# A decoder layer on one core: squares summed in PSUM, single-column threshold steps, key halves, query blocks and joining factors made one step ahead

## The chip, the cores and the metric

The kernel runs on one core of one Trainium2 chip. The metric is the device time of one execution in microseconds (us), lower is better. TensorE is called PE in the profile, VectorE is DVE, ScalarE is ACT, GpSimd is POOL, and SyncE, which issues nearly all transfers, is SP.

## The reference, cut to what matters

One inference step of one decoder layer, for a prompt of 1024 tokens and for 8 samples of 8 new tokens with 4096 cached tokens each (1088 tokens in all). The model width is 1024, the inner width of the feed-forward parts 2816.

```python
x = x + 0.5 * swiglu(rms_norm(x, g_ffn1), w1_gate, w1_up, w1_down)
mixed, state = mixer(rms_norm(x, g_mix) @ w_in)      # attention with chosen keys, and a short convolution
x = x + mixed @ w_out
x = x + 0.5 * swiglu(rms_norm(x, g_ffn2), w2_gate, w2_up, w2_down)
gate = sigmoid(rms_norm(x, g_ple) @ w_ple_gate)
x = x + gate * (pe @ w_ple_proj)                     # and a last rms_norm
```

In the mixer, an indexer gives every token a score for every earlier key, and each token attends only to its 256 best keys:

```python
score = einsum('bth,bthl->btl', w, relu(logits))
score = where(adm, score, -inf)
_, idx = top_k(score, topk)
o = softmax(q . k[idx] / 8) @ v[idx]                 # 8 query heads, 2 key heads of 64
```

## The kernel before

All activations lie transposed in SBUF, features on partitions and tokens along the row. The 1088 tokens are cut into three chunks `c`: chunks 0 and 1 of 288 tokens (together group a, tiles `xa`, `xna`) and chunk 2 of 512 tokens (group b, `xb`, `xnb`). Every fp32 operand of a large product is split into a high half (`hi`, a rounding to fp32r that ACT makes with a copy) and a low half (`lo`, the rest, a subtraction on POOL, sometimes on DVE), and three matmuls (L1421 to L1423) form one product. So each 128x1024 weight tile costs ACT one copy (L828) and POOL one subtraction (L728) before PE can use it.

The order of the work is one list of events written by `Plan.order()`. Each engine walks through the same list and issues its own share of every event, so the list sets the order of every engine's queue, and each engine runs its queue strictly in order, waiting on semaphores. The large products are the list's backbone. `weave(main, groups, first, last)` hangs groups of small events behind the product parts ("p") `first` to `last` of the backbone, spread evenly. A product of a 288-token chunk has 2 such parts of 12 matmuls, one of the 512-token chunk has 4 parts of 6 matmuls. The stages, in time:

- feed-forward 1 for chunks 0 and 1 (to about 485 us), then the input projection of group a. Woven into it are the indexer scores of the samples (events `sil`, `siw`, with the head matrix `wm` that they need) and the search for the 256th score of prompt blocks 2 and 3: `threshold_bit`, 32 steps, one bit of the threshold per step. A step counts on DVE, for both blocks, how many scores reach the candidate (L1224), and builds the next candidate from the counts with instructions of two columns (L1236, L1238) and one column (L1241).
- feed-forward 1 for chunk 2, into which are woven the rest of the samples' search (`sample_bit`) and the prompt attention of blocks 0 to 3 (`prompt()`), and then the attention of the samples (`samples()`).
- the output projection, the input projection of group b, and feed-forward 2 for chunks 0 and 1, with the searches B1 and B2 (blocks 4 to 7) and their attention.
- the rest of feed-forward 2, the last gate, the last norm.

A norm is a chain over four engines: ACT squares 8 row tiles (L837, L841), DVE adds them up (L1039), PE sums over partitions (`sums`, L1513), ACT takes the root (L850), DVE inverts it and writes it on diagonals (L1044, L1051), PE spreads these (`spread`, L1526), DVE scales x (L1057), ACT and POOL split the result. `norm(..., apart=True)` returns this chain in groups for `weave`.

In the prompt attention one unit is a block `b` and a head `r`. Over three steps of the list a unit goes through `qk` (PE logits into PSUM bank 5, DVE maximum L1328, ACT exponential L959), `ptr` (PE transposes, ACT copies them to `PT`, L966; DVE inverts the row sum and writes it on the diagonal `dg`, L1344 and L1347), and `pv` (PE values, and `dg` spread by a matmul L1629). The query halves of a block come from event `qb` (ACT L951, POOL `qb_lo` L756), which stands directly ahead of the block's first unit:

```python
            if now and now[1] == 0:
                groups.append([("qb", now[0])])
```

In the samples' attention there is one slot for each 256 keys of a pair of samples, 68 in all: PE logits (`kq`), transposes (`vt`, L1666) and values (`vp`, L1685); ACT copies the transposes (`PTs`, L990), makes the key's high half (`ks`, `K_hi`, L976), and POOL the low half (`kv_kr`, L778). Within a slot the events are sorted by rank; `ks` has rank 4, behind the slot's logits and transposes. `vo` joins four chunks (softmax factors over diagonals `diag_s`, L1389, spread by PE L1697).

The rotary step of the input projection (`rotate`) multiplies the product z in its PSUM bank by the cosine into an SBUF tile `tb` (L1108, after which the bank is free), multiplies the half-swapped copy by the sine (L1111), and adds the two SBUF tiles (L1119). PE has 3 banks for products in turn.

## Time and profile before

| | us |
|---|---|
| median of 3 runs (lowest, highest) | 3026.08 (3020.22, 3026.2) |
| profiled execution, its own time | 3023.26 |
| span of the profiled execution | 3021.5 |
| PE busy in the span | 2636.0 (87%) |
| DVE, POOL, ACT busy in the span | 1427.7, 1008.3, 1005.3 |
| mean granted clock of TensorE over the span | 0.937 |

Times in rows are microseconds, durations of one instruction nanoseconds. A row that ends in a bracket names how long the engine had been idle before it and whose instruction ended that. The granted clock (PEclk) is TensorE's, as a share of full speed; at 1.0 it is 2.4 GHz, and a stretch is either at that or at half, 1.2 GHz, so 0.9 means a fifth of the stretch at half.

### The profile page before, as it was taken

How to read it: one execution, taken by the hardware profiler on the slowest of the kernel's cores; microseconds unless marked ns; L12 is line 12 of the kernel's file. 1: busy time of each engine (PE TensorE's matmuls, PEld its weight loads, DVE VectorE, ACT ScalarE, POOL GpSimd, SP SyncE). 2: the span in 40 equal slices, each digit the busy share in tenths (PEclk: the TensorE clock that was granted, in tenths of full speed). 3: DMA queues.
4: the chain of work that ended last, by engine and by line, in shares of the span. 5: the costliest groups of instructions: out<-in, count | busy, mean ns of one | idle time of the engine just before them, and what ended most of it. 6: DMA issues, size and time to landing. Idle time of an engine off the chain costs nothing. (4 is left out here: it accounts for less than half of the span.)

```text
span 3021.5 us, 41472 instructions
## 1 busy us (share of the span) xinstructions
PE 2636.0 (87%) x15166; PEld 2285.3 (76%) x15166; DVE 1427.7 (47%) x3227; ACT 1005.3 (33%) x1581; POOL 1008.3 (33%) x521
## 2 busy tenths in 40 slices
PE   4999998787887878888898966888999999999997
PEld 4999998566666666666786656777889988778887
DVE  3233324679774212222366787776333343442354
ACT  4222224422333233332345312333444233332242
POOL 4333333223223333333344222122122344454341
PEclk9999998898898889998998978998999999999999
DMA  4333234221111333433142111111111323223222
GB/s 144 96 103 97 92 102 133 100 78 56 63 50 49 104 111 102 124 119 100 61 143 72 63 51 49 43 49 43 43 55 58 105 77 98 90 93 105 91 70 74
DMA packets 157038, 253.40 MB, mean 84 GB/s; under 512 B 15010, under 2 KB 101283, under 8 KB 156835
## 3 DMA queue, kind: packets, MB, share of 16 engines
q1 hardware_dynamic: 154144, 247.02, 25.4%
q10 hardware_dynamic: 2690, 3.72, 0.3%
q8 instruction: 121, 1.98, 0.3%
q14 instruction: 83, 0.67, 0.1%
HBM read 240.34 MB, written 18.73 MB: 86 GB/s over the span
## 5 line engine op out<-in xcount | busy, mean ns | idle before, releaser
L728 POOL TENSOR_TENSOR w_lo<-raw,w_hi 128x1024 fp32r<-128x1024 f32 x250 | 603.3, 2415 | 1075.9 <-ACT w_hi L828 1075.4
L1421 PE MATMUL ps<-xna_hi,w_hi 128*128 128x288 f32 x2000 | 614.2, 307 | 38.1 <-DVE tb L1133 14.1
L1422 PE MATMUL ps<-xna_lo,w_hi 128*128 128x288 f32 x2000 | 602.2, 301 | 0.0
L1423 PE MATMUL ps<-xna_hi,w_lo 128*128 128x288 f32 x2000 | 601.7, 301 | 0.0
L1421 PEld LDWEIGHTS ps<-xna_hi,w_hi 128*128 128x128 f32 x2000 | 389.5, 195 | 52.9 <-DVE tb L1133 14.7
L1421 PE MATMUL ps<-xnb_hi,w_hi 128*128 128x512 f32 x1000 | 420.1, 420 | 10.8 <-DVE tb L1133 5.7
L1422 PE MATMUL ps<-xnb_lo,w_hi 128*128 128x512 f32 x1000 | 403.9, 404 | 0.0
L1423 PE MATMUL ps<-xnb_hi,w_lo 128*128 128x512 f32 x1000 | 402.8, 403 | 0.0
L728 POOL TENSOR_TENSOR d_lo<-raw,d_hi 128x1024 fp32r<-128x1024 f32 x90 | 216.5, 2426 | 532.5 <-ACT d_hi L828 532.5
L1422 PEld LDWEIGHTS ps<-xna_lo,w_hi 128*128 128x128 f32 x2000 | 389.0, 194 | 0.2
L1423 PEld LDWEIGHTS ps<-xna_hi,w_lo 128*128 128x128 f32 x2000 | 388.0, 194 | 0.0
L828 ACT ACTIVATE w_hi<-raw 128x1024 fp32r<-128x1024 f32 x250 | 263.5, 1054 | 200.0 <-PE ps L1423 117.3
L1421 PE MATMUL ps<-ha_hi,d_hi 128*128 128x288 f32 x704 | 216.8, 308 | 30.4 <-DVE xa L1165 24.4
L1421 PEld LDWEIGHTS ps<-xnb_hi,w_hi 128*128 128x128 f32 x1000 | 198.1, 198 | 57.6 <-issue 8.5
L1423 PEld LDWEIGHTS ps<-xnb_hi,w_lo 128*128 128x128 f32 x1000 | 196.4, 196 | 44.1
L1422 PEld LDWEIGHTS ps<-xnb_lo,w_hi 128*128 128x128 f32 x1000 | 197.9, 198 | 36.6
L1422 PE MATMUL ps<-ha_lo,d_hi 128*128 128x288 f32 x704 | 209.2, 297 | 0.0
L1423 PE MATMUL ps<-ha_hi,d_lo 128*128 128x288 f32 x704 | 208.9, 297 | 0.0
L1165 DVE SCALAR_TENSOR_TENSOR xa<-ps,xa 128x288 f32<-128x288 f32 x352 | 156.6, 455 | 109.3 <-PE ps L1423 108.9
L1165 DVE SCALAR_TENSOR_TENSOR xb<-ps,xb 128x512 f32<-128x512 f32 x176 | 121.5, 691 | 171.1 <-PE ps L1423 170.8
L828 ACT ACTIVATE d_hi<-raw 128x1024 fp32r<-128x1024 f32 x90 | 90.9, 1052 | 325.5 <-PE ps L1423 297.5
L1074 DVE TENSOR_TENSOR ps<-silu_a,ps 128x288 f32<-128x288 f32 x88 | 40.6, 462 | 290.6 <-PE ps L1423 276.8
(288 smaller groups left out, 4236.6 us busy)
## 6 DMA issues: line engine op xcount, KB each, us to landing
raw<-in_w_gu SPq DMA_DIRECT2D x176, 512.0 KB, 3.5
raw<-in_w_d SPq DMA_DIRECT2D x88, 512.0 KB, 3.5
raw<-in_w_ring SPq DMA_DIRECT2D x74, 512.0 KB, 3.5
pages<-in_vk_pages SPq DMA_DIRECT2D x256, 128.0 KB, 2.6
idx_flat<-in_idx_pages SPq DMA_DIRECT2D x256, 32.0 KB, 2.1
idxp<-idx_flat SPq DMA_DIRECT2D x8, 1024.0 KB, 8.1
x_spill<-xa SPq DMA_DIRECT2D x1, 2304.0 KB, 8.9
xa<-x_spill SPq DMA_DIRECT2D x4, 576.0 KB, 6.2
```

Of the source, the lines that this page charges most:

```text
L728: g_.tensor_tensor(lo[slot][:, :, :], raw[l % 2][:, :, :], hi[slot][:, :, :].bitcast(f32), ALU.subtract).then_inc(lo_done, 1)
L828: A(hi[slot][:, :, :], raw[l % 2][:, :, :], ACT.Copy).then_inc(hi_done, 1)
L1074: v.tensor_tensor(z, silu[g][:, own(c)], z, ALU.mult).then_inc(hmul_done, 1)
L1165: v.scalar_tensor_tensor(out=x[g][:, m, own(c)], in0=ps[:, 3 + (i - 1) % 2, 0:CH[c][1]], scalar=0.5, in1=x[g][:, m, own(c)], op0=ALU.mult, ...
L1421: mm(out, shi, mhi, start=first, stop=False)
L1422: mm(out, shi, mlo, start=False, stop=False)
L1423: return mm(out, slo, mhi, start=False, stop=last)
```

## The change

- `norm(..., apart=True)` returns an empty group between `sums` and `spread`, so `spread` falls one group later.
- `prompt()`: a block's `qb` stands at the fifth unit (r = 4) of the block before; for the first block it stands three groups ahead of its first unit.
- `samples()`: `ks` has rank -1, so the next slot's key halves are made ahead of the slot's own work; the joining factors of `vo` become events `vw` and `vf`, two and three slots behind the last logits of the four chunks, where `vo` stays at six.
- `wm` moves behind the indexer scores of blocks 2 and 3.
- The squares: ACT writes the first one into PSUM bank 5, DVE adds the next six there and writes the last sum to SBUF. Four of the 15 norms keep the old way (`in_psum`).
- The diagonal `dg` is written by ACT (a copy of the identity with a factor) ahead of its copy of the transposes.
- `rotate` multiplies by the cosine in place in PSUM and adds from there; PE takes the bank again after the whole step (`rope_done`).
- `threshold_bit`: the 128x2 instruction that makes the candidate with the next bit is gone, the comparison works on single columns; `sample_bit` needs one instruction less.

```diff
@@ -172,7 +172,7 @@
-        groups = [[("sums", k, c)], [("spread", k, c)] + [("scale", k, c, m) for m in range(4)], [("scale", k, c, m) for m in range(4, KT)]]
+        groups = [[("sums", k, c)], [], [("spread", k, c)] + [("scale", k, c, m) for m in range(4)], [("scale", k, c, m) for m in range(4, KT)]]
@@ -184,8 +184,10 @@
             pv = [("pv", *two)] if two else []
-            if now and now[1] == 0:
-                groups.append([("qb", now[0])])
+            if s == 0:
+                groups += [[("qb", now[0])], [], []]
+            elif now and now[1] == 4 and now[0] + 1 in blocks:
+                groups.append([("qb", now[0] + 1)])
@@ -206,13 +208,15 @@
                 if i < 4 and (ch, i) != (15, 3):
-                    put(s, (4, ("ks", *divmod(4 * ch + i + 1, 4))))
+                    put(s, (-1, ("ks", *divmod(4 * ch + i + 1, 4))))
                 put(end + 1 + i, (3, ("vt", ch, i)))
                 put(end + 2 + i, (1, ("vp", ch, i)))
                 slot["vp", ch, i] = end + 2 + i
             put(end, (1, ("smax", ch)))
             put(end + 1 + n, (2, ("ov", ch)))
             if ch % 4 == 3:
+                put(end + 2, (5, ("vw", ch // 4)))
+                put(end + 3, (5, ("vf", ch // 4)))
@@ -238,8 +242,8 @@
         first = weave(self.in_proj(0), self.norm(1, 1, True), 0, 2)
-        side = [[("iw", 0)], [("prep",), ("wm",)]] + [[("isc", 2, h, 0), ("isc", 2, h + 1, 0)] for h in (0, 2)]
-        side += [[("isc", 3, h, 0), ("isc", 3, h + 1, 0)] for h in (0, 2)] + [[("sil", 0)]]
+        side = [[("iw", 0)], [("prep",)]] + [[("isc", 2, h, 0), ("isc", 2, h + 1, 0)] for h in (0, 2)]
+        side += [[("isc", 3, h, 0), ("isc", 3, h + 1, 0)] for h in (0, 2)] + [[("wm",)], [("sil", 0)]]
@@ -351,8 +355,6 @@
                         add("rope", t, c)
-                        if t != T_IK:
-                            add("in_dve", e[1])
@@ -577,6 +579,10 @@
+        def in_psum(k, c):
+            return (k, c) not in ((1, 2), (2, 1), (4, 0), (4, 1))
@@ -827,14 +833,18 @@
+            added_up = [0]
             def square(k, c, m):
-                i = n("sq", k, c, m)
                 g = GROUP[c]
                 x_final(act, k, c, m)
                 if m == 0:
                     if k:
                         wait(act, sums_done, n("sums", k - 1, c))
-                    A(ssq[g][:, own(c)], x[g][:, m, own(c)], ACT.Square).then_inc(sq_done, 1)
+                    if in_psum(k, c):
+                        wait(act, ssq_done, added_up[0])
+                        added_up[0] = n("ssq", k, c, KT - 1)
+                    A(ps[:, 5, 0:CH[c][1]] if in_psum(k, c) else ssq[g][:, own(c)], x[g][:, m, own(c)], ACT.Square).then_inc(sq_done, 1)
@@ -961,6 +971,11 @@
                 o, k = page_groups(b)[i]
+                if i == 0:
+                    u = n("pv", b, r)
+                    act.wait_ge(ri_done, u)
+                    wait(act, pv_done, u - 2)
+                    A(dg[:, r % 2, :], ident[:, 0, :], ACT.Copy, scale=ri[:, r % 2:r % 2 + 1]).then_inc(dg_done, 1)
@@ -1036,7 +1051,8 @@
                     dve.wait_ge(ssq_done, n("ssq", k, c, m - 1))
-                v.tensor_tensor(ssq[g][:, own(c)], ssq[g][:, own(c)], sq[(q - 1) % 3][:, 0:CH[c][1]], ALU.add).then_inc(ssq_done, 1)
+                so_far = ps[:, 5, 0:CH[c][1]] if in_psum(k, c) else ssq[g][:, own(c)]
+                v.tensor_tensor(so_far if m < KT - 1 else ssq[g][:, own(c)], so_far, sq[(q - 1) % 3][:, 0:CH[c][1]], ALU.add).then_inc(ssq_done, 1)
@@ -1105,7 +1121,7 @@
                 if t != T_IK:
-                    v.tensor_tensor(zt[:, own(c)], z, cos, ALU.mult).then_inc(in_dve, 1)
+                    v.tensor_tensor(z, z, cos, ALU.mult)
@@ -1116,7 +1132,7 @@
                     dst = iqT[g][:, t, own(c)] if t < T_IK else zt[:, own(c)] if t == T_K else attn[g][:, t - T_Q, own(c)]
-                    v.tensor_tensor(dst, zt[:, own(c)], zs[:, own(c)], ALU.add).then_inc(rope_done, 1)
+                    v.tensor_tensor(dst, z, zs[:, own(c)], ALU.add).then_inc(rope_done, 1)
@@ -1232,14 +1248,12 @@
                 count(hits if name != "B1" else early_hits if j < EARLY else late_hits, blocks, cand[:, :].bitcast(f32), ALU.is_ge)
-                if j < 31:
-                    v.tensor_scalar(with_bit[:, :], cand[:, :], 1 << (30 - j), None, ALU.bitwise_xor)
-                dve.drain()
-                v.tensor_scalar(drop[:, :], reached[:, :], TOPK - 0.5, 1.0 if j else -1.0, ALU.is_lt, ALU.mult)
                 dve.drain()
                 for i in range(2):
-                    v.tensor_scalar(cand[:, i:i + 1], drop[:, i:i + 1], 31 - j if j else 0, (with_bit if j < 31 else cand)[:, i:i + 1],
-                                    ALU.logical_shift_left, ALU.bitwise_xor)
+                    v.tensor_scalar(drop[:, i:i + 1], reached[:, i:i + 1], TOPK - 0.5, float(2 ** (31 - j)) if j else -1.0, ALU.is_lt, ALU.mult)
+                dve.drain()
+                for i in range(2):
+                    v.tensor_scalar(cand[:, i:i + 1], drop[:, i:i + 1], 1 << (30 - j) if j < 31 else 0, cand[:, i:i + 1], ALU.bitwise_xor, ALU.bitwise_xor)
@@ -1278,10 +1292,11 @@
                 dve.drain()
-                v.tensor_scalar(s_other[:, :], s_other[:, :], s_reached[:, :], None, ALU.add)
+                v.tensor_scalar(s_drop[:, :], s_other[:, :], s_reached[:, :], TOPK - 0.5, ALU.add, ALU.is_lt)
                 dve.drain()
-                v.tensor_scalar(s_drop[:, :], s_other[:, :], TOPK - 0.5, 1.0 if j else -1.0, ALU.is_lt, ALU.mult)
-                dve.drain()
+                if j == 0:
+                    v.tensor_scalar(s_drop[:, :], s_drop[:, :], -1.0, None, ALU.mult)
+                    dve.drain()
@@ -1341,10 +1356,8 @@
                 dve.wait_ge(exp_done, u)
+                wait(dve, dg_done, u - 2)
                 v.reciprocal(ri[:, s:s + 1], rs[:, s:s + 1]).then_inc(ri_done, 1)
-                dve.wait_ge(ri_done, u)
-                wait(dve, pv_done, u - 2)
-                v.tensor_scalar(dg[:, s, :], ident[:, 0, :], ri[:, s:s + 1], None, ALU.mult).then_inc(dg_done, 1)
@@ -1377,9 +1390,11 @@
-            def sample_out(p):
+            def sample_lowest(p):
                 dve.wait_ge(s_nbias, 4 * p + 4)
                 v.tensor_reduce(s_low[:, :], s_nb[:, p % 2, :], axis=AX.X, op=ALU.min).then_inc(s_lowest, 1)
+            def sample_shares(p):
@@ -1388,6 +1403,8 @@
+            def sample_out(p):
@@ -1441,6 +1458,8 @@
                 elif kind == "in":
+                    if key[0] < T_V and key[0] != T_IK:
+                        pe.wait_ge(rope_done, n("rope", key[0], c))
```

On DVE, in search B1 (the threshold steps of blocks 4 and 5 inside feed-forward 2; `small_i` holds the candidates), one step and the start of the next stood like this before:

```order
L1224 TENSOR_SCALAR hits_late,small<-score_131,small_i 128x640
L1224 TENSOR_SCALAR hits_late,small<-score_132,small_i 128x768
L1236 TENSOR_SCALAR small_i<-small_i 128x2
L1238 TENSOR_SCALAR small_i<-small 128x2
L1241 TENSOR_SCALAR small_i<-small_i 128x1 x2
L1224 TENSOR_SCALAR hits_late,small<-score_131,small_i 128x640
```

and now, with the line numbers of the changed kernel:

```order
L1240 TENSOR_SCALAR hits_late,small<-score_131,small_i 128x640
L1240 TENSOR_SCALAR hits_late,small<-score_132,small_i 128x768
L1253 TENSOR_SCALAR small_i<-small 128x1 x2
L1256 TENSOR_SCALAR small_i<-small_i 128x1 x2
L1240 TENSOR_SCALAR hits_late,small<-score_131,small_i 128x640
```

The two instructions of two columns have become two of one column.

On ACT, in the samples' attention, where the exponential (`Sa`) of a chunk stands in the middle, the order before was:

```order
L990 ACTIVATE PTs_126<-ps 128x256
L976 ACTIVATE K_hi_124<-pages 128x512
L982 ACT_TABLE_LOAD
L982 ACTIVATE Sa_181,small<-Sa_181,small 128x1024
L990 ACTIVATE PTs_125<-ps 128x256
L976 ACTIVATE K_hi_123<-pages 128x512
```

and at a like place now:

```order
L1005 ACTIVATE PTs_126<-ps 128x256
L991 ACTIVATE K_hi_123<-pages 128x512
L997 ACT_TABLE_LOAD
L997 ACTIVATE Sa_181,small<-Sa_181,small 128x1024
L1005 ACTIVATE PTs_125<-ps 128x256
L991 ACTIVATE K_hi_124<-pages 128x512
```

The tile number shows the move: `K_hi_123`, the key half for the next slot, stood behind the exponential and the slot's transposes (`PTs_125`) and stands ahead of both. POOL's queue is the same in these slots, weight halves included.

On POOL, at the last block of the first prompt attention (`qs` are the samples' queries, `w_lo` and `d_lo` weight halves), before:

```order
L728 TENSOR_TENSOR d_lo_76<-raw_64,d_hi_74 128x1024
L761 MEMSET qs_f 128x768
L767 COPY qs_f<-attn_a 64x4x8 x16
L770 CAST qs_hi<-qs_f 128x768
L772 TENSOR_TENSOR qs_lo<-qs_f,qs_hi 128x768
L756 TENSOR_TENSOR qb_lo_173<-attn_a,qb_hi_169 128x512
L728 TENSOR_TENSOR w_lo_71<-raw_63,w_hi_67 128x1024
```

and now:

```order
L734 TENSOR_TENSOR w_lo_72<-raw_64,w_hi_68 128x1024
L762 TENSOR_TENSOR qb_lo_173<-attn_a,qb_hi_169 128x512
L734 TENSOR_TENSOR w_lo_69<-raw_63,w_hi_65 128x1024
L767 MEMSET qs_f 128x768
L773 COPY qs_f<-attn_a 64x4x8 x16
L776 CAST qs_hi<-qs_f 128x768
L778 TENSOR_TENSOR qs_lo<-qs_f,qs_hi 128x768
```

The block's query half has moved past the samples' queries and a weight half.

## Rows read from the trace of the kernel before

**Rows 1.** The page's head and its line of the granted clock in 40 slices.

```profile
span 3021.5 us, 41472 instructions
PE 2636.0 (87%) x15166; PEld 2285.3 (76%) x15166; DVE 1427.7 (47%) x3227; ACT 1005.3 (33%) x1581; POOL 1008.3 (33%) x521
...
PEclk9999998898898889998998978998999999999999
```

**Rows 2.** PE's waits, whole span: us in total, times, longest us.

```profile
PE ps L1421 <- POOL kv_kr L778: 75.5, 47, 10.4
PE ps L1421 <- DVE small L1328: 46.6, 24, 7.2
PE ps L1526 <- DVE diag L1051: 41.8, 9, 11.3
PE ps L1421 <- POOL qb_lo L756: 31.7, 5, 13.9
...
PE ps L1421 <- DVE tb L1133: 19.8, 5, 7.7
...
PE ps L1542 <- DVE WT L1192: 9.8, 1, 9.8
PE ps L1697 <- DVE diag_s L1389: 9.8, 4, 5.7
```

**Rows 3.** Stages: length, busy PE, PEld, DVE, ACT, POOL, clock, DMA, GB/s.

```profile
542.00:640.00 98.00, 86.54 (x456) 57.37 (x457) 65.83 (x229) 38.60 (x76) 14.65 (x7) 0.91 0.29 105
640.00:745.00 105.00, 84.10 (x540) 79.60 (x538) 93.95 (x218) 24.18 (x33) 39.68 (x19) 0.90 0.18 61
745.00:950.00 205.00, 159.67 (x700) 121.46 (x701) 151.85 (x390) 66.41 (x122) 59.71 (x43) 0.88 0.16 53
...
1020.00:1500.00 480.00, 388.22 (x1978) 310.44 (x1979) 104.59 (x312) 155.17 (x245) 162.87 (x99) 0.89 0.36 108
...
1735.00:2120.00 385.00, 300.49 (x1871) 273.77 (x1872) 295.31 (x745) 114.95 (x172) 84.73 (x36) 0.87 0.14 46
```

**Rows 4.** Timeline of slots in the samples' attention: start, length, instruction.

```profile
1196.78 0.62 ACT L976 ACTIVATE K_hi<-pages 128x512 fp32r<-128x512 f32 x1
...
1197.48 1.27 POOL L778 TENSOR_TENSOR kv_kr<-pages,K_hi 128x512 fp32r<-128x512 f32 x1 [3.58 <-ACT K_hi L976]
1198.89 0.36 PE L1421 MATMUL ps<-K_hi,qs_hi 128*128 128x256 f32 x1 [1.04 <-POOL kv_kr L778]
```

**Rows 5.** Timeline of such a slot with two down weights on POOL.

```profile
1231.79 4.70 POOL L728 TENSOR_TENSOR d_lo<-raw,d_hi 128x1024 fp32r<-128x1024 f32 x2 [8.06 <-ACT d_hi L828]
...
1237.85 0.36 PE L1421 MATMUL ps<-K_hi,qs_hi 128*128 128x256 f32 x1 [2.36 <-POOL kv_kr L778]
```

**Rows 6.** Timeline of DVE and POOL in search B1.

```profile
1780.68 2.40 POOL L728 TENSOR_TENSOR w_lo<-raw,w_hi 128x1024 fp32r<-128x1024 f32 x1 [25.93 <-ACT w_hi L828]
...
1781.49 1.62 DVE L1236 TENSOR_SCALAR small_i<-small_i 128x2 int32<-128x2 int32 x1
...
1783.43 0.34 DVE L1241 TENSOR_SCALAR small_i<-small_i 128x1 int32<-128x1 int32 x2
```

**Rows 7.** Groups by form: count, busy us, mean ns of one, idle before.

```profile
L1039 DVE TENSOR_TENSOR ssq_a<-ssq_a,sq 128x288 f32<-128x288 f32 x70 | 73.2, 1045 | 49.7 <-ACT sq L841 47.3
...
L1074 DVE TENSOR_TENSOR ps<-silu_a,ps 128x288 f32<-128x288 f32 x88 | 40.6, 462 | 290.6 <-PE ps L1423 276.8 <-ACT silu_a L869 12.9
...
L1236 DVE TENSOR_SCALAR small_i<-small_i 128x2 int32<-128x2 int32 x93 | 36.2, 389 | 0.0
...
L1241 DVE TENSOR_SCALAR small_i<-small_i 128x1 int32<-128x1 int32 x192 | 32.1, 209 | 8.7 <-issue 1.7
L1347 DVE TENSOR_SCALAR dg<-ident,small 128x128 f32<-128x128 f32 x64 | 31.2, 488 | 2.3
...
L1238 DVE TENSOR_SCALAR small_i<-small 128x2 int32<-128x2 f32 x96 | 29.8, 311 | 7.3
```

**Rows 8.** Timeline: a norm's spread inside feed-forward 2.

```profile
2582.68 1.65 PE L1526 MATMUL ps<-diag,ones 128*128 128x128 f32 x6 [4.93 <-DVE diag L1051]
```

More of the change, by code:

```diff
@@ L424, in program @@
         s_w, s_f = small[:, 28:32], small[:, 32:36]
-        cand, with_bit, drop = [small_i[:, 2 * j:2 * j + 2] for j in range(3)]
+        cand, drop = [small_i[:, 2 * j:2 * j + 2] for j in range(2)]
         s_cand, s_with_bit, s_drop = [small_i[:, 6 + j:7 + j] for j in range(3)]
@@ L1012, in _ @@
                     "sil": sample_logits, "siw": sample_scores, "vtr": values, "qb": queries, "qk": logits, "ptr": transposed,
-                    "ks": keys, "smax": weights, "vt": sample_transposed, "vo": shares, "mix": mix, "pe": embed}
+                    "ks": keys, "smax": weights, "vt": sample_transposed, "vw": shares, "mix": mix, "pe": embed}
             for e in events:
```

2 lines of the change are left out of this document (1 added, 1 removed).

## The prediction

> **What bounds the kernel now.** I first read the page's head and PE's waits. PE is busy for 2636.0 of 3021.5 us [rows 1]; it is idle for 385 us, and nothing else is near its bound, so time can only come from PE's idle time and from its clock. The waits say who holds PE up [rows 2]: POOL's key halves 75.5 us, the DVE maximum of the attention logits (L1328) 46.6, the diagonals of the norms 41.8, the query halves 31.7, DVE's convolution step (L1133) 19.8, the head matrix 9.8 and the joining factors 9.8. The stages [rows 3] say where: 92 us of idle time in the samples' attention (480 less 388.2), 85 in search B and its attention (385 less 300.5), 78 in 542 to 950. In the last two DVE is busy for 0.76 of the time (295.3 of 385, 311.6 of 408); in the samples' attention only for 0.22, so there it is a chain, not an engine's load. The clock [rows 1, 3] is the second loss: the granted clock of these stages is 0.87 to 0.91. At 0.89, a share of 0.22 of 480 us runs at 1.2 GHz, 106 us, and what PE does in it takes twice as long.
>
> **Key halves.** In an ordinary slot of the samples' attention, `K_hi` runs behind ACT's copy of the transposes (1196.78, 0.62), then POOL's `kv_kr` (1197.48, 1.27), and PE's next logits start at 1198.89, after 1.04 us of idleness [rows 4]. With `ks` ahead of the slot's own work, `K_hi` of the next slot runs behind the copy of the slot before, a whole slot earlier. Its key pages must be there (they come four slots ahead) and its buffer is free (its last reader is the slot before). PE's list of such stalls has 22 of 1.03 to 1.05 us, 4 of 1.74 or 1.75 where the exponential stands in the way, and 3 under 0.5: 31 us in all. The other 18 have another cause, which stays: POOL is at a weight. In [rows 5] two `d_lo` hold it until 1236.49, and `kv_kr` can't start earlier whatever ACT does; PE still waits its 2.36. There are 9 of these (2.36 to 3.42, 23 us), 8 of 1.27 to 1.53 behind one `w_lo`, and the first, 10.4, waits for the first pages. I take 31 off; the bounds are 20 (pages come late where slots get shorter) and 45 (half of the `w_lo` and `d_lo` ones go too).
>
> **Joining factors.** `vw` and `vf` now stand three to four slots ahead of their spread; slots are near 5 us. The 9.8 us go but for 1: 8.5, bounds 4 and 10.
>
> **Norms.** `spread` falls later behind `sums`: by one part of 6 matmuls in the two norms of the first input stage of group b, by 12 in the one before, and in feed-forward 2 from 18 matmuls to 36 and to 48. A matmul of 512 columns at full clock takes 0.21 us, so that is 1.3, 1.3, 2.6, 3.8 and 6.4 us of cover. [rows 8] is one of two stalls of 4.93 us. I take off 1.3 + 2.6 + 3.8 + 4.9 = 12.6, bounds 8 and 16. The norms at both ends of the kernel have no product between, and the second one of the first input projection only moves its wait to the scaled tiles.
>
> **Head matrix.** Five groups later its 9.8 us are covered; some of it may come back as a wait for the indexer keys, since these loads don't start earlier. 9, bounds 0 and 10.
>
> **Query halves.** Of 31.7 us [rows 2], the longest, 13.9, is block 4's; it gets two groups more (some 4 us), but its `qb_hi` on ACT stands behind a product that waits for DVE's tie steps. The other four, 17.8 in sum, belong to blocks that now have four units' lead, one of them past the samples' queries on POOL (the order above). 4 + 15 = 19, bounds 12 and 28.
>
> **DVE's threshold steps and diagonals.** The 128x2 instructions take 389 and 311 ns on average, the 128x1 209 [rows 7]. [rows 6] shows why the averages are high: L1236 takes 1.62 us and ends as POOL's `w_lo` ends (1783.08). The Trainium skill (SBUF — State Buffer, "Who interferes with whom") says that DVE and GpSimd share a port pair under an exclusive lock, which a tensor_scalar in a two-port mode takes and one outside it doesn't; the trace agrees as far as L1241, which is never slow. So a step saves 0.39 + 0.31 less the 0.34 of a pair of single columns [rows 6], 0.36, and with 96 steps 35 us, of which I put three quarters in search B, where it has 64 of the steps and POOL is at weights beside them. The samples' search loses one single-column instruction, 0.21 x 32 = 7. `dg` takes 0.49 from DVE in each of 64 units; blocks 0 to 2 are in 745 to 950 (24 units, 12 us), blocks 4 and 5 in search B's stage (16 units, 8 us). So DVE is lighter by 9 + 7 + 12 = 28 us before 950 and by 26 + 8 = 34 in search B. PE's idle time there was 78 and 85 us [rows 3]. Not all of DVE's gain arrives, since PE and DVE take turns in waiting: I take 20 and 25 (near three quarters), bounds 7 and 9 (a quarter), and 28 and 40 (all, with the drains that go).
>
> **What costs or gains nothing.** `dg` on ACT costs 64 instructions of some 0.3 us in a queue that is busy for 0.32 in 745 to 950 [rows 3]; DVE itself took 0.49 [rows 7]; it waits for the reciprocal, which DVE makes right behind the maximum that ACT's exponential needs anyway, and PE needs the transposes only one unit later. The squares: 77 adds with one operand from PSUM should go from 1045 ns (L1039, [rows 7]) to the 462 of L1074, 45 us of DVE; but they lie in stages in which PE is full, and only the last sums wait for them, 3 us (bounds 0 and 5). The Trainium skill speaks against this step (VectorE: DVE Perf Modes, "The TRN2 errata — SBUF-src ops pay a fixed extra latency per instruction": 120 against 58 cycles of fixed cost for a PSUM source). By it the 77 adds would take 5 us more, on nobody's path; the row of L1074 shows no such price. The rotary step holds PE's bank for two DVE instructions more, some 1 us of the two products (6 us) until PE is back at it; its third instruction loses its contention, in a stage in which PE is full.
>
> **Clock.** These terms take 128 of 385 us of idleness, a third. The granted clock of 0.937 over the span means some 380 us at 1.2 GHz, and it falls where PE stalls: slices 1 to 6 of the page's line, feed-forward 1, hold 9. If a fifth of these 380 us returns to 2.4 GHz, PE saves half of it: 39, bounds 12 and 75.
>
> **Sum.** 31 + 8.5 + 12.6 + 9 + 19 + 20 + 25 + 3 + 39 = 167. The profiled execution took 3023.26 us with a span of 3021.5; the median is 3026.08. 3026 - 167 = 2859. All the low bounds together give 72 (2954), all the high ones 257 (2769).
>
> **Rivals.** (1) The stalls are handed on: what DVE and the key halves no longer hold up waits for the next in line, POOL's weights (L728 stands in front of `kv_kr` and `qb_lo` alike), DVE's tie steps, or the key pages on SP. For it: POOL's weights are what PE waits for in [rows 5]. Then the key halves, the joining factors and the head matrix keep 31 + 8 + 9, DVE brings a quarter (16), the clock 12, the rest 10: 86, 2940. Against it: in [rows 4] nobody but the chain itself is late, and POOL had been idle for 25.93 us ahead of the weight in [rows 6]. (2) The clock returns further. If it comes back for half of the 380 us, that is 95 instead of 39, and all of DVE's gain arrives (+17): 167 + 56 + 17 = 240, 2786. Against it: the stalls behind weights remain, 34 us in the samples' attention alone. (3) Slower: `dg` holds up ACT. ACT's queue is in order; if the reciprocal stands behind a threshold step of DVE (two counts and their tail, near 2.7 us in search B), `PT`, the silus and the weight copies behind `dg` all wait. At 2.7 us for each of 64 units that is 173, and 64 x 0.3 = 19 for the copies: 167 - 192, so 3051. It decides from (167 - 19) / 64 = 2.3 us a unit up; against it stands the order above: in the list the reciprocal follows the maximum directly, and the threshold step is ahead of both. (4) The change does not do what it says on DVE: single columns still take the port, PSUM adds are no faster. Then 45 and 3 are gone, and with them 8 of the clock: 111, 2915, inside my range.
>
> **Chances and range.** My forecast 0.74, rival 1 with rival 4 0.16, rival 2 0.07, rival 3 0.02, no difference 0.01. Two runs of this kernel can differ by 0.2% (6 us), which is about what a measurement can tell from no change. Cases 1, 2 and 4 are all faster. Faster by over 0.2%: 0.96, within 0.01, slower 0.03. The range 2768 to 2950 takes in rivals 1, 2 and 4 and leaves out little more than the ends of the bounds.
>
> **What the changed profile would show.** The wait of PE for `kv_kr` at 45 us, all of 1.2 us and more; for `diag_s` under 2; for `qb_lo` near 13; no stall of 4.93. The squares' adds near 0.46 us, the new single-column instructions at 0.15 to 0.21 with no slow ones, DVE's busy time down by some 120 to 1300 us. Mean granted clock near 0.95. The forecast is wrong if the samples' attention (480 us [rows 3]) is not shorter by 40 or more with the clock, or if search B's stage (385) does not lose 45; and if PE's waits show a new name, ACT's `PT` or `rope_done` above all.

## The result: 2951, where 2859 was predicted

The changed kernel takes 2951.43 us (median of 4 runs, 2947.79 to 2952.68), the kernel before 3026.14 (4 runs); ratio 0.9755, 95% interval 0.9738 to 0.9772. That is 75 us faster where 167 was predicted, and 1.4 us outside the range. The page of the changed kernel, to compare with [rows 1]:

```profile
span 2946.0 us, 41473 instructions
...
PE 2630.5 (89%) x15166; PEld 2293.6 (78%) x15166; DVE 1307.1 (44%) x3135; ACT 1020.3 (35%) x1641; POOL 1010.6 (34%) x521
...
PEclk9999998999889989888999988999999999999999
```

PE's idle time fell from 385.5 to 315.5 us, by 70 (the prediction took 128 off). PE's busy time, in which a faster clock would show, fell by 5.5 where 39 was forecast: over the span the time at 1.2 GHz went from 379 to 349 us, where 76 was to go. DVE lost 121 us, as foretold. PE's waits, to compare with [rows 2]:

```profile
PE ps L1438 <- POOL kv_kr L784: 59.2, 21, 10.3
PE ps L1438 <- DVE small L1343: 54.6, 15, 13.3
PE ps L1545 <- DVE diag L1067: 43.7, 12, 11.2
...
PE ps L1438 <- DVE tb L1149: 11.6, 4, 5.5
...
PE ps L1438 <- POOL qb_lo L762: 3.4, 1, 3.4
...
PE ps L1586 <- DVE Wm L1214: 1.2, 1, 1.2
```

Names have gone or shrunk (`diag_s` is no longer there, `WT` neither, `qb_lo` was 31.7), but the DVE maximum rose from 46.6 to 54.6, the diagonals by 2, and `kv_kr`, forecast at 45, stands at 59: fewer stalls (21 for 47) that are longer each (18 of the 21 take 2 us or more, 10 of the 47 did).

These stages are cut at the same instruction in both kernels: the prompt attention of blocks 0 to 3, the samples' attention, and the stage from group b's input projection to the end of search B's attention, before (length, busy PE, PEld, DVE, ACT, POOL, clock, DMA share, GB/s):

```profile
752.06:1029.07 277.01, 228.33 (x1040) 174.50 (x1040) 169.60 (x433) 95.27 (x165) 80.00 (x52) 0.90 0.18 57
1029.07:1527.70 498.63, 413.78 (x2103) 331.48 (x2103) 123.06 (x333) 166.90 (x261) 170.11 (x100) 0.91 0.36 110
...
1613.48:2441.98 828.50, 729.68 (x4417) 638.71 (x4417) 501.31 (x1179) 295.45 (x433) 225.00 (x98) 0.94 0.18 59
```

and after:

```profile
751.54:1009.42 257.88, 224.79 (x1022) 172.35 (x1022) 145.42 (x365) 105.45 (x197) 85.48 (x52) 0.90 0.19 61
1009.42:1489.48 480.06, 419.14 (x2103) 346.02 (x2103) 125.38 (x333) 163.96 (x259) 169.59 (x100) 0.88 0.38 114
...
1575.29:2368.88 793.59, 718.04 (x4411) 629.53 (x4411) 437.79 (x1146) 300.12 (x459) 223.68 (x98) 0.95 0.19 61
```

Two of these cuts moved with the change itself: block 0's first logits and group b's first `spread` now stand 18 and 6 weight matmuls further down the list (x1040 became x1022, x4417 x4411). So blocks 0 to 3 lost 19 in these rows, but with the stage ahead of them, which got 4 longer, 15; search B lost 35, or 32 between the same weight matmuls. The stretch of 1735 to 2120, for which the prediction asked 45, lost 26 by that cut (383.5, then 357.1), and the samples' attention 19, where 40 was the mark. In that last one PE idles 24 us less (84.9, then 60.9) and is busy for 5 us more with the same 2103 matmuls, at a lower clock (0.91, then 0.88).

**The key pages.** The prediction let `K_hi` be read a slot earlier on the ground that its pages "come four slots ahead". ACT's waits before, and after, say what that did:

```profile
ACT K_hi L976 <- DMA pages<-in_vk_pages: 15.4, 8, 7.3
```

```profile
ACT K_hi L991 <- DMA pages<-in_vk_pages: 84.9, 25, 7.2
```

One such case in the changed kernel's timeline (start, length, instruction, idle time before it; the last row is another slot, for the clock below):

```profile
1047.61 0.34 SPq L609 DMA_DIRECT2D raw<-in_w_gu  x1
1053.26 8.66 SPq L692 DMA_DIRECT2D pages<-in_vk_pages  x12
...
1058.01 0.63 ACT L991 ACTIVATE K_hi<-pages 128x512 fp32r<-128x512 f32 x1 [5.57 <-DMA pages<-in_vk_pages]
...
1058.71 1.27 POOL L784 TENSOR_TENSOR kv_kr<-pages,K_hi 128x512 fp32r<-128x512 f32 x1 [8.66 <-ACT K_hi L991]
...
1060.12 0.36 PE L1438 MATMUL ps<-K_hi,qs_hi 128*128 128x256 f32 x1 [2.19 <-POOL kv_kr L784]
...
1206.91 0.36 PE L1438 MATMUL ps<-K_hi,qs_hi 128*128 128x256 f32 x1 [2.36 <-POOL kv_kr L784]
```

SP issues a weight transfer at 1047.61, when POOL is done with that buffer, then reads the 16 page numbers of the next chunk into registers, and only at 1053.26 issues the first page: over 5 us in which SP issues no transfer. ACT stands at `K_hi` for 5.57 us, POOL is idle for 8.66, PE waits 2.19.

The kernel before shows that there was little room. By its list a key tile's pages are issued three slots ahead of its logits in 44 of 60 cases, not four: the transfer waits until PE is done with the values of the tile eight before it, which have the same buffer. And in its trace the pages of the first key tile after a reading of page numbers had landed 0.9 us before `K_hi` began (medians, the first eight tiles left out), those of the other three 3.6 to 5.9 us. A slot takes some 6 us. In the changed kernel these are 0.0 and 1.2 to 2.9, and 63 of the 73 us that ACT waits for these tiles stand at the tiles behind a reading.

**The clock.** Before, a stall of 1.04 us at 1198.89 [rows 4] left the clock alone:

```profile
1191.00:1197.80 6.80, 5.06 (x29) 3.70 (x27) 0.72 (x3) 2.46 (x6) 1.58 (x2) 1.00 0.43 126
1197.80:1205.00 7.20, 5.12 (x33) 4.01 (x32) 1.88 (x5) 2.36 (x4) 2.22 (x2) 1.00 0.26 75
```

After, the clock fell behind the stall of 2.36 us that ends at 1206.91:

```profile
1200.00:1204.50 4.50, 4.50 (x28) 3.53 (x26) 0.77 (x3) 3.14 (x5) 3.65 (x2) 1.00 0.10 13
...
1208.00:1214.80 6.80, 6.80 (x26) 5.65 (x26) 0.51 (x3) 0.39 (x1) 0.00 (x1) 0.53 0.24 73
```

From 1208.00 to 1214.80 the granted clock is near its lower level (1.2 GHz) and PE needs the whole stretch for 26 matmuls, where it had 28 in 4.5 us; those of 512 columns, which had followed each other by 0.23 us, now do so by 0.43. I counted PE's stalls in the samples' attention and a little around it, cut at the same weight matmuls: before, 42 of 0.8 to 2 us and 12 of 2 us or more, with 102 us at 1.2 GHz; after, 7 and 19, with 123 us. Below, "the stage" is this cut.

### The profile page after: what moved, and what is told of

Same layout as the page of the kernel before. It is cut to its first block, busy times and chain, and to the rows that moved or that the text cites. A ratio compares the mean times of both kernels' runs of the same rounds, so it can differ in the third digit from the quotient of the medians.

```text
span 2946.0 us, 41473 instructions
## 1 busy us (share of the span) xinstructions
PE 2630.5 (89%) x15166; PEld 2293.6 (78%) x15166; DVE 1307.1 (44%) x3135; ACT 1020.3 (35%) x1641; POOL 1010.6 (34%) x521
## 4 chain that ended last, share of the span: by engine, by line
PE 69%; DVE 15%; ACT 4%; issue 4%; POOL 3%; DVEq 2%; DMA 2%; SPq 1%; ACTq 0%
PE ps L1438 21%; PE ps L1439 19%; PE ps L1440 19%; PE ps L1646 2%; PE ps L1704 2%; POOL w_lo L734 2%; DVE hits L1240 1%; PE ps L1632 1%; DVE hits_early L1240 1%; DVE ps L1090 1%; DVE s_hits L1288 1%; ACT w_hi L834 1%; DVE ha_lo L1092 1%; PE ps L1573 1%; DVE tb L1154 1%
## 5 line engine op out<-in xcount | busy, mean ns | idle before, releaser
L1438 PE MATMUL ps<-ha_hi,d_hi 128*128 128x288 f32 x704 | 215.6, 306 | 22.2 <-DVE xa L1181 21.1
```

The lines of the kernel that those rows point to most:

```text
L1438: mm(out, shi, mhi, start=first, stop=False)
```

## Experiments

18 kernels, four or five runs each (12 of k_alone, 11 of n_before), beside the kernel before on the same chip (its medians there are 3026.5 to 3027.3). "Faster" and "slower" are against the changed kernel's 2951.4 unless another is named. The 95% intervals are 4 to 7 us wide to either side for most kernels, so a difference under some 6 us is not told from none. Idle is span less PE's busy time in the profiled execution, which is one of the runs and not always near the median.

| kernel | median (range) | PE busy | PE idle | mean clock |
|---|---|---|---|---|
| changed | 2951.4 (2947.8-2952.7) | 2630.5 | 315.5 | 0.941 |
| u_keys | 2953.0 (2949.5-2955.9) | 2625.4 | 328.7 | 0.944 |
| u_steps | 2988.2 (2968.0-2997.4) | 2627.7 | 338.5 | 0.940 |
| u_dg | 2959.7 (2947.6-2960.4) | 2632.8 | 325.3 | 0.940 |
| u_norm | 2949.5 (2941.2-2950.9) | 2631.9 | 317.2 | 0.939 |
| u_qb | 2952.9 (2937.9-2960.4) | 2638.8 | 319.7 | 0.938 |
| u_psum | 2966.6 (2964.3-2969.0) | 2640.2 | 322.3 | 0.938 |
| u_joins | 2964.4 (2961.0-2965.7) | 2634.3 | 328.3 | 0.936 |
| k_alone | 3017.8 (3011.6-3027.8) | 2645.6 | 370.9 | 0.933 |
| n_before | 3018.4 (3016.7-3021.1) | 2632.4 | 382.7 | 0.939 |
| n_after | 2929.2 (2927.3-2929.7) | 2615.3 | 312.5 | 0.945 |
| f_weights | 2940.0 (2935.9-2942.6) | 2618.8 | 322.1 | 0.941 |
| f_numbers | 2912.7 (2911.6-2922.5) | 2610.3 | 310.4 | 0.944 |
| k_numbers | 2972.1 (2965.9-2979.6) | 2616.9 | 347.2 | 0.947 |
| f_all | 2913.8 (2909.6-2916.8) | 2616.8 | 298.0 | 0.945 |
| f_late | 2947.8 (2944.6-2949.8) | 2639.1 | 307.8 | 0.939 |
| f_pages | 2980.4 (2979.2-2981.3) | 2624.9 | 353.7 | 0.936 |
| f_hold1 | 2960.0 (2950.9-2962.7) | 2609.4 | 348.9 | 0.940 |
| k_weights | 2984.3 (2980.8-2985.6) | 2624.4 | 359.0 | 0.941 |

### One part undone at a time

**u_keys.** 

> The changed kernel with the rank of ks put back from -1 to 4, all else as changed (2951). My theory: key halves one step ahead removed only the stalls of 1.04 and 1.75 us, and these cost no clock, while the stalls behind POOL's weights grew, so the edit is worth what the waits say: kv_kr goes from 59 back to about 75, 16 us, 2967 (2961 to 2973). Rival: the edit brought its full 31 us and something else took 15 away: 2982. Rival: the stalls behind weights simply take over, nothing is gained: 2951 to 2955.

```diff
-                    put(s, (-1, ("ks", *divmod(4 * ch + i + 1, 4))))
+                    put(s, (4, ("ks", *divmod(4 * ch + i + 1, 4))))
```

1.5 us slower, no difference: in the range of the last rival. Idle time rose by 13, PE's wait for `kv_kr` is back at 74.9 as I expected, and busy time fell by 5; the stage has 38 short stalls, 11 of 2 us or more and 92 us at 1.2 GHz, for 123. The waits said 16, the time says nearly nothing: the theory had the waits right and the price wrong, since with the edit undone 8 long stalls go too, and with them 31 us at 1.2 GHz.

**u_steps** (`threshold_bit` and `sample_bit` as before). 

> The changed kernel with the old instructions of two columns in threshold_bit and the old sample_bit. DVE gets 35 + 7 us busier. As the prediction priced it (three quarters arrive): about 30 us, 2981. My theory now: PE's idle time in search A and B hangs on DVE only in a few places (the first logits of block 4, of block 0, some maxima), so a third to a half arrives: 12 to 20 us, 2963 to 2971. Rival: DVE's slower steps are hidden and nothing arrives: 2951 to 2956.

37 slower in the median, above all I expected. The five runs spread over 29 us, with mean clocks from 0.940 down to 0.932; the profiled one is the fastest of them (2968.0), and its span is 20 above the changed kernel's, 23 more of idle time and 3 less of busy time. So 23 is what the profile shows of waiting, and how much of the 37 is the clock is not shown by a trace. PE's waits for `tb` and the DVE maximum, 11.6 and 54.6, are 19.6 and 67.3.

**u_dg** (`dg` on DVE as before). 

> The changed kernel with the diagonal dg written by DVE again. DVE gets 31 us busier (64 x 0.49). Priced in the prediction as three quarters of 12 + 8 us in the places where PE waits for DVE, 15 us less what ACT's copies cost: 2961 to 2966. Rival: DVE is not the last there and ACT's dg costs PE something (its waits for ACT's PT are 14 us): 2945 to 2951.

8 slower, with runs from 2947.6 to 2960.4; idle time rose by 10, as PE's wait for the maxima did (54.6, then 65.2).

**u_norm.**

```diff
-        groups = [[("sums", k, c)], [], [("spread", k, c)] + ...
+        groups = [[("sums", k, c)], [("spread", k, c)] + ...
```

> The changed kernel without the empty group in norm(), so spread falls where it fell before. Prediction's term: 12.6. By the two profiles (diagonals 41.8 before, 43.7 after; 4.93 became 3.58, 4.93 became 1.44, 4.49 became 2.48, but 3.74, 1.90 and 1.40 are new or moved) I now expect 5 to 8 us of idle time, 2954 to 2960. Rival: the full 12.6, 2964. Rival: nothing, the empty group only moves the waits: 2948 to 2953.

Nothing lost, as the second rival said. Undone, the two stalls of [rows 8]'s kind are back:

```profile
2511.53 1.65 PE L1545 MATMUL ps<-diag,ones 128*128 128x128 f32 x6 [4.93 <-DVE diag L1067]
...
2606.72 1.38 PE L1545 MATMUL ps<-diag,ones 128*128 128x128 f32 x6 [4.93 <-DVE diag L1067]
```

In the changed kernel they are shorter by 4.8, but the norm at 2806 has a stall of its own that u_norm lacks:

```profile
2508.05 1.65 PE L1545 MATMUL ps<-diag,ones 128*128 128x128 f32 x6 [3.58 <-DVE diag L1067]
...
2599.78 0.94 PE L1545 MATMUL ps<-diag,ones 128*128 128x128 f32 x6 [1.44 <-DVE diag L1067]
...
2806.41 2.08 PE L1545 MATMUL ps<-diag,ones 128*128 128x128 f32 x8 [3.74 <-DVE diag L1067]
```

DVE's rows ahead of that stall say why:

```profile
2796.36 0.18 DVE L1060 RECIPROCAL rstd<-rstd 128x4 f32<-128x4 f32 x1 [0.77 <-ACT rstd L860]
2802.78 0.46 DVE L1102 TENSOR_TENSOR ps<-silu_a,ps 128x288 f32<-128x288 f32 x1 [6.24 <-PE ps L1440]
...
2803.66 2.70 DVE L1067 TENSOR_SCALAR diag<-ident,rstd 128x128 f32<-128x128 f32 x4
```

The empty group moved not PE's `spread` alone but DVE's share of the event too: the diagonals, for which all was ready at 2796.54, now stand behind the additions of the next product, which wait for PE for 6.24 us. The prediction's list of norms did not have this one. Three more got worse with the empty group: at 501 a stall of 1.28 is 3.73, and those of 1.40 at 1497 and 1.90 at 2897 are new. In all PE waits 43.7 us for these diagonals, 39.8 with the group gone.

**u_qb** (`qb` directly ahead of the block's first unit). 

> The changed kernel with qb put back ahead of each block's first unit, and without the two empty groups. The four query halves at 745 to 950 (17.8 us before, gone after) come back, the one of block 4 (13.9) only changes its name (13.3 + 3.4 after, for DVE and for qb_lo). Theory: 15 of the prediction's 19 are real, 2963 to 2970. Rival: DVE's maxima take them over (PE's wait for small rose by 8): 2955 to 2960.

1.5 slower, and the runs go from 2937.9 to 2960.4, so no difference can be read. The rival's mechanism is there, though not its 4 to 9 us: most of what goes from one line comes up on the other (63.4 together, 58.0 in the changed kernel):

```profile
PE ps L1436 <- DVE small L1341: 31.9, 14, 7.0
PE ps L1436 <- POOL qb_lo L760: 31.5, 5, 13.9
```

**u_psum** (`in_psum` always false). 

> The changed kernel with all sums of squares in SBUF again. DVE gets 77 x 0.5 = about 40 us busier where PE is full. Prediction's term: 3, so 2954. Rival: nothing, 2949 to 2953. Rival: the late norms (diagonals, and the sums at the kernel's ends) gain more from it than I gave them: 2958 or more.

15 slower, the third case: the profile has 7 us more of idle time and 10 more of busy time, with 369 us at 1.2 GHz in the span for 349.

**u_joins** (`vw`, `vf` and `wm` at their old places). 

> The changed kernel with the joining factors and the head matrix at their old places. PE's waits for diag_s (9.8) and WT (9.8, now Wm 1.2 and rl 2.1) come back: idle time up by 15 to 18, 2966 to 2970 if the clock stays. Rival (their gain was given to the next in line): 2951 to 2957.

13 slower, a little under what I expected, with 13 more of idle time. `diag_s` (10.8) and `WT` (9.9) are back.

The seven differences (1.5, 37, 8, -2, 1.5, 15, 13) add up to 74 of the 75 us. With some 5 us of noise in each that is no proof that they act independently, and the key halves below show that one of them does not. The rotary step was not tried alone.

### The key halves and SP

**f_pages.** Two edits of SP's queue (from both, cut to what matters): it reads the next chunk's numbers right behind the last pages of this one, and it keeps a weight's transfer back until the slot's pages are issued, which puts 28 of this stage's 29 weight transfers behind one more slot's pages:

```diff
-                if k % 4 == 0:
+                if k == 0:
                     numbers[:] = page_numbers(4 * k, 16)
...
+                if k % 4 == 3 and k < 63:
+                    numbers[:] = page_numbers(4 * k + 4, 16)
...
+                if e[0] == "sp" and ks_seen and numbers:
+                    pending.append(e)
...
+                if pending and (e[0] == "kl" or not ks_seen):
+                    for q in pending:
+                        does["sp"](*q[1:])
```

> The changed kernel (2951), only SP's queue in the samples' attention altered: the pages' transfers of a slot are issued ahead of the weight transfers that fall into it, and the 16 page numbers of a chunk are read as soon as the registers are free. Theory C (the key halves gain nothing because K_hi, read a slot earlier, waits for its pages: ACT's wait for pages rose from 15 to 85 us with the change, and the halves made late then meet POOL's weights): ACT's wait for pages falls under 30, PE's wait for kv_kr from 59 to about 45, the time by 10 to 15 with it: 2936 to 2941. Rival A (POOL's weights in front of kv_kr alone): ACT's wait falls, PE's does not, 2948 to 2954. Theory D, on the clock, holds beside either: what PE's idle time loses in this stage comes back for the most part as time at 1.2 GHz, so the gain is under half of the idle time saved.

29 slower, outside both ranges. ACT's wait for pages fell to 36, but ACT now waits 56 us for the raw weight (`d_hi`), and PE's wait for `kv_kr` rose to 84. SP issues pages and weights from one queue, and here the one that stood behind came late.

**f_hold1** (as f_pages, a weight's splitting a slot later). 

> As f_pages, and the splitting of a weight in this stage stands a slot later in the list, behind the next slot's keys and pages, so that POOL's kv_kr does not stand behind it and ACT's d_hi does not block K_hi. If the two causes together (pages late, weights in front) make up all that the key halves should have brought, PE's wait for kv_kr falls to 10 to 20 (10 is the first), idle time by 40, and the time is 2911 without help of the clock, 2890 if the clock returns with it, and 2930 or more if theory D holds (the clock takes back half or more).

9 slower. PE's wait for `kv_kr` did not fall to 20 but rose to 93; raw weights are late again (61 us), and the stage idles 104 us in fewer and longer stalls.

**k_weights** (as f_pages, keys at rank 4, a weight's splitting behind `ks`). 

> As f_pages, but the keys at their old rank (4), and the weights' splitting behind the slot's ks. Then every slot has the short stall of about 1.04 us (some 45 us in all with the first), no long one behind a weight, and the pages have their full lead. Theory D (long stalls and work without pauses both bring PE to 1.2 GHz, short stalls do not): PE's idle time is about that of the changed kernel less 15 to 25, with less time at 1.2 GHz in the stage than its 115 us: 2925 to 2940. Rival (the key halves a step ahead are worth their 31 us once pages and weights are out of the way): slower than f_hold1 by 20 or more.

33 slower. It is 24 behind f_hold1, as the rival said, which speaks for a worth of the keys' lead once the queues are out of its way. Every variant that puts pages ahead of weights on SP lost against the changed kernel.

**f_weights.** The splitting (with its next transfer) stands behind the next `ks`; on SP only 4 of the stage's 29 weight transfers fall behind one more slot's pages:

```diff
-            out.append(("sp", len(self.items) - 1))
+            (held if holding else out).append(("sp", len(self.items) - 1))
...
             out.append(e)
+            if e[0] == "ks":
+                out += held
+                held, holding = [], e[1:] != (15, 3)
```

> The changed kernel, but in the samples' attention a weight's splitting (ACT w_hi and d_hi, POOL w_lo and d_lo) is written into the list behind the next ks instead of ahead of it, so kv_kr no longer stands behind a weight that PE itself has just released. Theory A (queue order is the cause of what was left of the key halves): PE's wait for kv_kr falls from 59 to about 15, of which the first 10 stays; 44 us of idleness go, 2907, and if the clock returns for half of the stage's 115 us at 1.2 GHz, another 25: 2880. Rival B (the weights themselves are the late ones, POOL's work in a slot doesn't fit in PE's): the wait changes its name to d_lo or w_lo and the time stays within 10 us: 2941 to 2960.

11 faster, neither theory: PE's wait for `kv_kr` is 55 and not 15, idle time rose by 7, busy time fell by 12, and ACT's wait for pages rose to 135 us. Theory A, that POOL's order alone was the cause, fell here.

**k_alone** (the kernel before, `ks` at rank -1, nothing else). 

> The kernel before (3026) with the key halves' edit alone (rank -1). Theory C: ACT's wait for pages rises from 15 to 80 or more, the stalls of 1.04 us go, stalls of 2 us and more go from 12 to about 19 in this stage, and the time hardly moves: 3018 to 3028. Rival (prediction's term, if nothing else of the change disturbed it): 2995.

9 faster than the kernel before (ratio 0.9974, 0.9963 to 0.9986), not 31. PE's wait for `kv_kr` and ACT's for the pages:

```profile
PE ps L1421 <- POOL kv_kr L778: 59.9, 20, 10.4
...
ACT K_hi L976 <- DMA pages<-in_vk_pages: 80.0, 26, 7.3
```

The stage has 143 us at 1.2 GHz for 102, 19 stalls of 2 us or more for 12, and 9 shorter ones for 42. So the pages were late by this edit alone, and nothing else of the change was needed to take most of the gain away.

**n_after** and **n_before**: the four lines on the page numbers above, alone, in the changed kernel and in the one before. 

> The changed kernel (2951) with the early page numbers alone. Theory C: the pages come some 5 us earlier once in four keys, ACT's wait for pages falls from 85 to about 60, two or three of the 19 long stalls go: 2930 to 2944. Rival (only both edits together help, the weights stand in front): 2947 to 2953.

 

> The kernel before (3026) with the early page numbers alone. Theory C: its keys are made a slot later and find their pages there (ACT's wait for pages is 15 us in all), so nothing changes: 3020 to 3029. Rival (SP is late for everything, weights too): 3010 or less.

22 faster in the changed kernel; in the one before 8 faster than that kernel, a little more than the nothing that I expected (ratio 0.9974, 0.9965 to 0.9983), with 3 us less of idle time. SP's order of transfers is the same in n_after as in the changed kernel. Its waits:

```profile
PE ps L1440 <- POOL kv_kr L786: 49.8, 17, 10.4
...
ACT K_hi L993 <- DMA pages<-in_vk_pages: 59.1, 27, 7.3
```

**f_numbers** (f_weights and the page numbers). 

> f_weights (2940) with one thing more: SP reads the 16 page numbers of the next chunk right behind the last pages of this one, instead of ahead of the next pages (it spends 5 us on them each time, and K_hi waits: ACT's wait for pages is 135 us in f_weights). Theory C, SP's queue is what the key halves now wait for: ACT's wait for pages under 90, PE's wait for kv_kr from 55 to 25 to 35, 2915 to 2930 with the clock as it is. Rival (theory D has the upper hand): idle time falls, the time by less than half of it: 2930 to 2938. Rival (SP is not it): 2938 to 2942.

39 faster than the changed kernel, ratio to the kernel before 0.9624 (0.961 to 0.9637): the stage is down to 10 stalls of 2 us or more and 87 us at 1.2 GHz.

```profile
PE ps L1445 <- POOL kv_kr L791: 34.4, 11, 10.7
...
ACT K_hi L998 <- DMA pages<-in_vk_pages: 100.4, 30, 7.6
```

Faster than I expected, though ACT's wait is not under 90. It is PE's that counts: against n_after, whose only difference is the order of the splitting, PE's wait for `kv_kr` is 15 less and the time 17.

**k_numbers** (f_numbers with `ks` back at rank 4). 

> f_numbers (2913) with the rank of ks put back from -1 to 4. Theory C: the term of 31 us was right for a kernel whose pages are in time. Then the stalls of 1.04 us come back, some 40 us in all, without as many long ones: 2935 to 2945. Rival (the keys' lead never mattered, f_numbers gains by SP's numbers alone): 2910 to 2918.

59 slower than f_numbers. PE waits 92 us for `kv_kr`, and the stage has 40 stalls of 0.8 to 2 us. Neither range held. The 59 is not the keys' lead alone: this kernel is also 19 slower than u_keys, from which it differs by the early numbers and the splitting, and at this rank the splitting follows directly on the keys. u_keys with the early numbers alone was not tried. If they gave it the 8 that they gave the kernel before, it would take 2945, and the lead would be worth 16 against n_after; that is an estimate, and the lead's own worth is not shown.

### Block 4's first logits

The stall of 13.29 us, where 13.9 for `qb_lo` had been, in the changed kernel:

```profile
1799.72 0.56 DVE L1278 TENSOR_SCALAR score<-score 128x768 f32<-128x768 f32 x1
...
1800.54 1.15 DVE L1240 TENSOR_SCALAR_CACHE_REDUCE hits<-score,small_i 128x896 bf16<-128x896 f32 x1
...
1814.07 0.33 DVE L1256 TENSOR_SCALAR small_i<-small_i 128x1 int32<-128x1 int32 x2
...
1814.52 0.49 DVE L1343 CUSTOM_DVE_ANT_0 Sx_b<-ps,score 128x320 f32<-128x320 f32 x1
...
1815.07 0.63 PE L1438 MATMUL ps<-kT_hi,qb_hi 64*128 64x320 f32 x1 [13.29 <-DVE small L1343]
```

The tie steps end at 1800.28, and then four steps of search B2 run before the maximum (the rows show the first count and the last step's end): three of them were given the place of `qb` and of the two empty groups behind it.

**f_late.**

```diff
-            side.append((late[i] if i < len(late) else []) + g)
+            side.append((late[i - 4] if 4 <= i < len(late) + 4 else []) + g)
```

> The changed kernel, but search B2's steps start four groups later, so that no threshold step stands between the tie steps of search B1 and the first logits of block 4 on DVE (now four stand there, some 13 us). Theory: PE's stall of 13.3 us at 1815 shrinks to about 2, and with it goes some of the 20.5 us at 1.2 GHz there: 2951 - 11 - 8 = 2932; a part comes back as blocks 4 and 5 see four steps more later: 2932 to 2943. Rival: the logits wait for the tie steps anyway, nothing changes: 2948 to 2953.

4 faster, less than the range and within the noise. The 300 weight matmuls around block 4's first logits take 10 us less, but the 300 around 2020 take 8 more: B2's tie steps for block 6 now stand ahead of the last maximum of block 5, and PE has a stall of 7.00 us at 2025.99. Idle time fell by 8, busy time rose by 9. **f_all** (f_numbers with two groups instead of four). 

> f_numbers (2913) with search B2's steps two groups later, so that two threshold steps instead of four stand between B1's tie steps and the first logits of block 4. The stall of 13.3 us shrinks by 6, and by f_late (8 us of idle time less brought 4): 2905 to 2911. Rival: the steps come to stand ahead of block 6 and cost there what they save: 2911 to 2915.

No difference to f_numbers, as its rival said: the medians are 1 us apart. The profile has 12 us less of idle time and 6 more of busy time, but f_numbers' profiled run is the slowest of its five (2922.5).

## Why the prediction was wrong

- **Key halves: 31 forecast, 2 measured.** The failing step is "Its key pages must be there (they come four slots ahead)". By the kernel's own list they come three slots ahead of the logits in 44 of 60 cases, and the first tile behind a reading of page numbers had 0.9 us to spare where the move asked for a slot, some 6. I named pages as a low bound (20) and read no wait of ACT or of SP for it. The 22 stalls did vanish; the halves came late by another way, behind SP and then behind POOL's weight, as stalls of over 2 us. k_alone shows it without the rest of the change: 9 us instead of 31, ACT's wait for pages 80 instead of 15. That SP had its part is shown by n_after (22 us from the page numbers alone, against 8 in the kernel before, whose keys are made later); that the order of the weights had its part, by f_numbers against n_after (17 us).
- **Clock: 39 forecast, 5.5 of busy time measured.** "It falls where PE stalls" was right, "if a fifth of these 380 us returns to 2.4 GHz" had no ground: 30 us returned. The idleness that went was for the most part in short stalls, behind which the clock had not fallen. In 14 of the profiles together (the two kernels and the twelve variants that were run first), I counted the stalls near which time at 1.2 GHz began, from 1 us ahead of the stall to 4 us behind it:

  | stall, us | stalls | with a fall of the clock |
  |---|---|---|
  | 0.8 to 1.2 | 340 | 30 |
  | 1.2 to 2 | 225 | 75 |
  | 2 to 2.5 | 167 | 140 |
  | 2.5 to 4 | 312 | 275 |
  | 4 to 6 | 110 | 109 |

  Seen from the other side, 615 of the 706 falls stand at a stall of 2 us or more and none away from every stall (two stand at one under 0.8), so the half of theory D by which work without pauses would bring the clock down too is not borne out.
- **Query halves: 19 forecast, 1.5 measured, and norms: 12.6 forecast, nothing (both within the noise).** Both steps counted what PE gets as cover and did not look at DVE's queue at the new place. Rival 1 had the mechanism ("waits for the next in line, ... DVE's tie steps"); of block 4 the prediction named the obstacle and still took off 4 us.
- **Joining factors and head matrix: 17.5 forecast, 13 measured.** Right but for the size: 18 of 19.6 us of waits went, and 13 arrived.
- **DVE's steps and diagonals: 45 forecast, 37 + 8 measured.** The mechanism is right, the equal number is luck: 45 was meant as idle time alone, of which the two profiles show 23 + 10, and the 37 has runs 29 us apart. New single columns take 149 ns, the adds 466 as foretold; `dg` on ACT takes 397, where I had put some 0.3 us. The Trainium skill (SBUF — State Buffer, "Who interferes with whom") lets an instruction with at most one SBUF input, outside the two-port modes, pass beside GpSimd, and the trace agrees: no single-column form has a raised mean. The dearer PSUM source that the Trainium skill gives (VectorE: DVE Perf Modes, "The TRN2 errata — SBUF-src ops pay a fixed extra latency per instruction") is not in this trace: an add of 512 columns took 699 ns with one operand in PSUM and 689 with both in SBUF, in the one norm of that width that keeps the old way. At 288 columns it took 466 ns with one in PSUM and 1197 with both in SBUF, beside POOL's weights.

The rows (groups by form: count, busy us, mean ns of one):

```profile
L1256 DVE TENSOR_SCALAR small_i<-small_i 128x1 int32<-128x1 int32 x192 | 32.2, 209 | 7.8 <-issue 0.6
...
L1055 DVE TENSOR_TENSOR ssq_a<-ssq_a,sq 128x288 f32<-128x288 f32 x21 | 25.1, 1197 | 13.7 <-ACT sq L851 13.7
L1253 DVE TENSOR_SCALAR small_i<-small 128x1 int32<-128x1 f32 x192 | 20.7, 149 | 8.1 <-issue 0.9
...
L1055 DVE TENSOR_TENSOR ps<-ps,sq 128x288 f32<-128x288 f32 x42 | 19.6, 466 | 37.5 <-ACT sq L851 35.5
...
L1055 DVE TENSOR_TENSOR ps<-ps,sq 128x512 f32<-128x512 f32 x24 | 16.8, 699 | 37.2 <-ACT sq L851 37.0
...
L1055 DVE TENSOR_TENSOR ssq_b<-ssq_b,sq 128x512 f32<-128x512 f32 x7 | 4.8, 689 | 1.0 <-ACT sq L851 0.7
...
L978 ACT ACTIVATE dg<-ident,small 128x128 f32<-128x128 f32 x64 | 25.4, 397 | 90.5 <-DVE small L1360 90.3
```

- **Squares in PSUM: 3 forecast, 15 measured.** "Only the last sums wait for them" was nearly right for idle time (7 us: undone, PE's waits for the sums rise from 27.6 + 2.8 to 29.9 + 6.3 and for `xa` from 21.1 to 23.5); the other 8 go with 19 us more at 1.2 GHz, which the term left out. Its 45 us of DVE were near the 48 of u_psum by luck: not 77 adds are of 288 columns but 49, and the 28 of 512 columns went from 1417 to 699 ns.

Each measured term has its own share of the clock in it, and each is good to some 5 us. By this account, of the 92 us that were missing 39 are the clock, 29 the key halves, 18 the query halves, 14 the norms and 4 the joins, less 12 for the squares. The outcome is nearest to rival 1 (2940), with other contents: what it gave up on DVE arrived in full, and what it kept of the key halves did not.

## What to carry to other kernels

Before making a step earlier, read what its inputs wait for in the order of time, on the queue that issues them too: here a wait of 15 us became 85 and most of the gain was gone. Price a stall by what the clock does behind it: with 35 short stalls gone and 7 more long ones, the samples' attention had 24 us less of idle time and some 20 more at 1.2 GHz. Look at the queue of every engine that takes part in an event that is moved, not only at the one that waited. Reading an address table while a queue is waiting anyway was the cheapest edit of all, 22 us in the changed kernel.

## What the runs showed that I had not expected

The samples' attention has the same list of instructions in u_steps, u_dg and the changed kernel, and nearly the same idle time (67, 71 and 71 us), yet it took 485, 507 and 503 us (cut as for the counts of stalls), with 90, 133 and 123 us at 1.2 GHz. So what the clock takes in a stage was not set by the stage's own instructions and idle time alone; on what else it depends no run shows. A term below some 10 us can't be read from one profile. The kernel u_steps itself spread over 29 us from run to run, at mean clocks from 0.932 to 0.940. And SP needs over 5 us for 16 page numbers, in which it issues no transfer at all.
